# Layer 0's opening by halves of the features: the first modulation, x and the input weights in two halves, with four weight units between them

## The chip, the cores and the metric

The kernel runs on one core of one Trainium2 chip. The metric is the device time of one execution in microseconds (us); the figure compared is the median of the runs. A profile is one execution recorded by the hardware, with every instruction's start and end on TensorE (PE), VectorE (DVE), ScalarE (ACT), GpSimd (POOL) and the DMA queues.

## The reference

It is a two-layer decoder trunk in fp32 with 256 tokens and 1024 features. What matters here is the start of layer 0:

```
mod = silu(c) @ w_ada[l] + b_ada[l]          # 1024 x 6144 per layer
shift1, scale1, gate1, shift2, scale2, gate2 = split(mod, 6)
h = x * (1 + scale1) + shift1
z = h @ w_in                                 # 1024 x 1984: q 256, kv 128, key 64, then 3 x 512 channels
...                                          # attention from the first 448, gated conv from the channels
y = concat(rms(attn), rms(conv)) @ w_o
x = layer_norm(alpha * x + gate1 * y)
h = x * (1 + scale2) + shift2
f = swiglu(h)  (layer 0)   or   top-2 of 8 experts  (layer 1)
x = layer_norm(alpha * x + gate2 * f)
```

## The kernel before

All weights stream through a ring of seven slots of 2 MB in SBUF, `raw[0..6]`. The order of the loads is the list `loads`; the SyncE queue issues them in that order (L486 to L492) and waits, for each, until the load seven places earlier has been released by its reader. `w_ada` comes as strips `("ada", l, n)` of 512 rows by one vector of 1024 columns, two strips for each of the six vectors of a layer; `w_in` comes as `wa` (the 448 columns of the attention inputs) and as `wb`, `wc`, `wu` (512 channel columns each); then come `qkv`, `oc` and `oa`.

Modulation. VectorE multiplies each strip row block (128 rows by 1024 columns) by a per-partition value of silu(c) and adds it to an accumulator `ada_acc` (`ada_part`, L1063, the instruction at L1082; the text calls one of them a sum). The accumulator begins as the bias, written by ScalarE (`ada_init`, L648). After the eight sums of a vector TensorE adds over the partitions: by one-column products (`early_sums`, L1749) for the first two vectors, by a product with ones for the gates (L1731), by transposes (L1729) for the others, whose blocks ScalarE then adds up (`drain_ada`, L660). The results pass one after another through PSUM bank 7, in the order of the list `BANK7`. For strips 1 and 2 TensorE also takes over the fourth row block (`early_rows`, L1742). `unread` issues eight products of 512 columns (L1756) whose results nobody reads.

After both vectors, TensorE turns x (`turn_input`, L1773), ScalarE and VectorE modulate it into `h_t` (L682, L1100), and TensorE forms the low-rank part with `wa` in fp32 (L1815). The channel blocks are formed from two-part splits: for each of twelve weight units (128 x 1024) ScalarE makes the high part in one of three buffers `w_mix` (L732), VectorE the low part (L1187), and TensorE does 24 products (`channels`, `three`, L1794 to L1796), after which the buffer is free. The same is done for the modulated input in two halves (`halve`: L739, L1192). VectorE's stream has in between: an angle table (L1153 to L1168), the scaling by the norms and the rotary key (L1217 to L1226), and the strip sums of the later vectors, placed by hand with `sums`. After the units come the product `cu` (L1241), convolution, scores (L1898), softmax, the output products for the conv rows (L1918) and the attention rows (L1957), and the feed-forward, whose first product is L1971.

Of the kernel before, what the change touches and what calls it, by code (L numbers as in the profile page):

```python
# [28 lines left out]
P = 128  # L29
# [52 lines left out]
BANK7 = [("ada", 0, 0, 0), ("ada", 0, 1, 0), "params"]  # L82
PE_ROWS = (1, 2)
BANK7 += [("ada", 0, 2, 0), ("ada", 0, 2, 1), ("ada", 0, 3, 0), ("ada", 0, 3, 1), ("ssq_conv", 0), ("ssq_attn", 0), ("ada", 0, 4, 0), ("ada", 0, 4, 1)]
# [13 lines left out]
HALVED = EARLY + 1  # L98

MIX_UNITS = 12  # L100
MRING = 3
MIX_ADA = (((5, 6), (7,), (8, 9)), ((), (9, 10), (11,)))
MIX_FIRST, MIX_LATE = ((4, 5, 6, 7), (9,)), ((8, 9), (10, 11))
# [23 lines left out]
def trunk(nc, a, out):  # L127
    with ExitStack() as ctx:
# [5 lines left out]
        def sem(name):  # L134
# [32 lines left out]
        c_col = sb("c_col", [P, KC])  # L167
# [95 lines left out]
        hx_hi, hx_lo = (hx_hi0, hx_hi1), (hx_lo0, hx_lo1)  # L263
        rp_k = cu[:, 0, 2:].rearrange("p (k t r) -> p k t r", k=4, t=TT)
# [38 lines left out]
        half_full = [sem(f"half_full{k}") for k in range(HALVED)]  # L303
# [4 lines left out]
        prm_loaded, x_loaded, ln_loaded, rt_loaded = (sem("prm_loaded"), sem("x_loaded"), sem("ln_loaded"),  # L308
                                                      sem("rt_loaded"))
# [49 lines left out]

        def win_src(l, lo, hi):  # L360
            return a["w_in"][l][:, lo:hi].rearrange("(c p) n -> p c n", p=P)
# [3 lines left out]
        def load_ada(l, n):  # L365
            k = ADA_ORDER.index(("ada", l, n))
            src, parts = strip_src(l, n), 2 if k < EARLY else 1
            loads.append((("ada", l, n), [(q * SLOT // parts, (q + 1) * SLOT // parts, 4 // parts,
                                           src[:, q * 4 // parts:(q + 1) * 4 // parts, :]) for q in range(parts)],
                          (bank7_full, BANK7.index(("ada", l, n // 2, 0)) + 1) if k < EARLY else (ada_summed, k + 1)))  # L370

# [3 lines left out]
        for n in range(4):  # L375
            load_ada(0, n)
        for l in range(L):
            z0 = ZA
            if l == 0:
                load_pe(("wa", l), [(h * 4 * ZA, (h + 1) * 4 * ZA, 4, win_src(l, 0, ZA)[:, 4 * h:4 * h + 4, :]) for h in range(2)],  # L380
                        (za_mm, TT * (l + 1)))
            else:
                load_pe(("wa", l), [(0, KC * ZA, KC, win_src(l, 0, ZA))], (za_mm, TT * (l + 1)))
            load_pe(("wb", l), [(0, SLOT, KC, win_src(l, z0, z0 + D_CONV))], (mix_used, MIX_UNITS * l + 4))
            if l == 0:
                load_ada(0, 4)
            load_pe(("wc", l), [(0, SLOT, KC, win_src(l, z0 + D_CONV, z0 + 2 * D_CONV))], (mix_used, MIX_UNITS * l + 8))
            for n in MIX_ADA[l][0]:
                load_ada(l, n)
            load_pe(("wu", l), [(0, SLOT, KC, win_src(l, z0 + 2 * D_CONV, z0 + 3 * D_CONV))], (mix_used, MIX_UNITS * l + 12))  # L390
            for n in MIX_ADA[l][1]:
                load_ada(l, n)
            load_pe(("qkv", l), [(0, 2 * 768, 2, a["w_uq"][l].rearrange("(c p) n -> p c n", p=P)),
                                 (2 * 768, 2 * 768 + 1024, 1, a["w_ukv"][l].rearrange("(c p) n -> p c n", p=P))], (v_mm, l + 1))
            for n in MIX_ADA[l][2]:
                load_ada(l, n)
            load_pe(("oc", l), [(0, SLOT, 4, a["w_o"][l][512:1024, :].rearrange("(c p) n -> p c n", p=P))],
                    (yc_mm, 3 * (l + 1)))
            load_pe(("oa", l), [(0, SLOT, 4, a["w_o"][l][0:512, :].rearrange("(c p) n -> p c n", p=P))],
                    (ya_mm, 2 * TT * (l + 1)))  # L400
            if l == 0:
# [55 lines left out]
        def chunk_ready(v, t, c):  # L457

            if v >= 1 and t == 0:
                return ht_ready, HT[v] + c + 1  # L460
# [169 lines left out]
        def _(act):  # L630
# [85 lines left out]
            def mixer(l):  # L716
# [9 lines left out]
                def unit(n):  # L726
                    name, at, g = mix_weight(l, n)
                    if at == 0:
                        wait_load(act, name)
# [1512 lines left out]
```

## Time and profile before

| | |
|---|---|
| median of 3 runs | 1418.36 us (1417.6 to 1418.51) |
| span of the profiled execution | 1415.7 us |
| TensorE busy | 1390.7 us |
| VectorE busy | 1251.7 us |
| ScalarE busy | 1012.6 us |
| HBM read | 475.67 MB, 340 GB/s over the span |

The profiled execution's own time is not given apart from its span; the span runs from its first to its last instruction and is 2.7 us below the median of the runs. All moments in the text are in us from the start of the span. A busy engine is one with an instruction in flight; idle time carries the name of what ended it.

### The profile page before, as it was taken

The numbers are of one execution on the slowest core, as the hardware profiler recorded it, in microseconds if no ns is written. First come the engines' busy times: TensorE is split into PE (matmuls) and PEld (weight loads), VectorE is DVE, ScalarE is ACT, GpSimd is POOL, SyncE is SP. The second block draws the span as 40 slices with busy tenths as digits, with TensorE's granted clock in tenths as the row PEclk, the third lists the DMA queues.
The fourth block names the chain that finished last, engine by engine and source line by source line (L and its number), as shares of the span: only waits on it lengthen the run. The fifth ranks groups of instructions, "written<-read, shape, count | busy, mean of one in ns | idle before, by whom it ended". The sixth has DMA issues, their size and how long they took to land.

```text
span 1415.7 us, 20150 instructions
## 1 busy us (share of the span) xinstructions
PE 1390.7 (98%) x7013; PEld 1149.1 (81%) x7013; DVE 1251.7 (88%) x1388; ACT 1012.6 (72%) x1286; POOL 63.3 (4%) x123
## 2 busy tenths in 40 slices
PE   6999999999999999999999999999999999999996
PEld 4876999997967888888888888888888888888885
DVE  5987888876799989998998899999889899899998
ACT  2453544454355888888988888888898888888884
POOL 1000000000013500000000000000000000001000
PEclk9999999999999999999999999999999999999998
DMA  9996398977564999999999999999999999999970
GB/s 361 416 412 240 143 349 290 378 282 276 207 258 171 385 369 366 392 380 375 379 393 365 366 398 367 380 383 387 367 379 392 365 371 392 387 362 390 413 306 32
DMA packets 203472, 482.16 MB, mean 341 GB/s; under 512 B 6944, under 2 KB 31630, under 8 KB 203418
## 3 DMA queue, kind: packets, MB, share of 16 engines
q1 hardware_dynamic: 198848, 470.31, 88.1%
q0 software_dynamic: 1584, 5.77, 1.0%
q10 hardware_dynamic: 2986, 5.38, 1.0%
q8 instruction: 32, 0.52, 0.1%
q14 instruction: 22, 0.18, 0.0%
HBM read 475.67 MB, written 5.77 MB: 340 GB/s over the span
## 4 chain that ended last, share of the span: by engine, by line
PE 96%; DVE 2%; DMA 1%; ACT 0%; issue 0%; POOL 0%; SPq 0%; ACTq 0%; DVEq 0%; POOLq 0%
PE ps L1794 27%; PE ps L1796 27%; PE ps L1795 27%; PE ps L1957 2%; PE ps L2144 2%; PE ps L1815 2%; PE ps L1918 2%; PE ps L1971 1%; PE ps L1756 1%; DMA raw<-in_w_ada_dram 1%; PE ps L1731 1%; PE ps L1867 0%; PE ps L2094 0%; PE ps L1773 0%; PE ps L1729 0%; PE ps L1898 0%
## 5 line engine op out<-in xcount | busy, mean ns | idle before, releaser
L1424 DVE TENSOR_TENSOR low<-raw,w_hi 128x1024 fp32r<-128x1024 f32 x448 | 531.6, 1218 | 24.4 <-ACT w_hi L853 16.2
L853 ACT ACTIVATE w_hi<-raw 128x1024 fp32r<-128x1024 f32 x448 | 470.2, 1061 | 84.3 <-PE ps L1796 79.4
L1795 PE MATMUL ps<-low,h_hi 128*128 128x512 f32 x904 | 351.9, 389 | 0.0
L1794 PE MATMUL ps<-w_hi,h_lo 128*128 128x512 f32 x680 | 269.5, 396 | 0.0
L1796 PE MATMUL ps<-w_hi,h_hi 128*128 128x512 f32 x680 | 265.3, 390 | 0.0
L1795 PE MATMUL ps<-low,hid_hi 128*128 128x512 f32 x528 | 205.7, 390 | 0.0
L1795 PEld LDWEIGHTS ps<-low,h_hi 128*128 128x128 f32 x904 | 169.9, 188 | 34.2
L1424 DVE TENSOR_TENSOR low<-raw,e_hi 128x1024 fp32r<-128x1024 f32 x112 | 136.7, 1220 | 19.8 <-ACT e_hi L853 19.8
L1796 PEld LDWEIGHTS ps<-w_hi,h_hi 128*128 128x128 f32 x680 | 127.6, 188 | 27.4
L1794 PEld LDWEIGHTS ps<-w_hi,h_lo 128*128 128x128 f32 x680 | 127.8, 188 | 24.9
L1424 DVE TENSOR_TENSOR low<-raw,hx_lo 128x1024 fp32r<-128x1024 f32 x112 | 136.5, 1219 | 3.7
L853 ACT ACTIVATE hx_lo<-raw 128x1024 fp32r<-128x1024 f32 x112 | 118.8, 1061 | 26.4 <-PE ps L1796 26.2
L1082 DVE SCALAR_TENSOR_TENSOR ada_acc<-raw,c_act,ada_acc 128x1024 f32<-128x1024 f32 x94 | 120.5, 1283 | 10.6 <-ACT ada_acc L648 8.3
L853 ACT ACTIVATE e_hi<-raw 128x1024 fp32r<-128x1024 f32 x112 | 118.8, 1061 | 10.0 <-PE ps L1796 10.0
L1795 PEld LDWEIGHTS ps<-low,hid_hi 128*128 128x128 f32 x528 | 99.2, 188 | 19.7
L1794 PE MATMUL ps<-h_hi,low 128*128 128x256 f32 x320 | 92.7, 290 | 0.0
L1796 PE MATMUL ps<-h_hi,w_hi 128*128 128x256 f32 x320 | 90.5, 283 | 0.0
L1795 PE MATMUL ps<-h_lo,w_hi 128*128 128x256 f32 x320 | 90.5, 283 | 0.0
L1794 PE MATMUL ps<-w_hi,hid_lo 128*128 128x512 f32 x224 | 87.9, 392 | 0.0
L1796 PE MATMUL ps<-w_hi,hid_hi 128*128 128x512 f32 x224 | 87.2, 389 | 0.0
L1351 DVE TENSOR_TENSOR h_t<-ps,sil 128x512 f32<-128x512 f32 x67 | 46.1, 688 | 26.7 <-PE ps L1796 14.1
L1795 PEld LDWEIGHTS ps<-h_lo,w_hi 128*128 128x128 f32 x320 | 61.3, 191 | 1.1 <-issue 1.0
(377 smaller groups left out, 2268.0 us busy)
## 6 DMA issues: line engine op xcount, KB each, us to landing
raw<-in_moe_w_gate_dram SPq DMA_DIRECT2D x56, 2048.0 KB, 8.5
raw<-in_moe_w_up_dram SPq DMA_DIRECT2D x56, 2048.0 KB, 8.6
raw<-in_moe_w_down_dram SPq DMA_DIRECT2D x56, 2048.0 KB, 8.7
raw<-in_w_ada_dram SPq DMA_DIRECT2D x20, 2048.0 KB, 12.7
raw<-in_w_in_dram SPq DMA_DIRECT2D x6, 2048.0 KB, 12.5
raw<-in_ffn_w_gate_dram SPq DMA_DIRECT2D x11, 1024.0 KB, 8.3
raw<-in_ffn_w_up_dram SPq DMA_DIRECT2D x11, 1024.0 KB, 10.9
raw<-in_ffn_w_down_dram SPq DMA_DIRECT2D x11, 1024.0 KB, 4.9
```

Of the source, the lines that this page charges most:

```text
L853: act.activation(e_hi[k % ERING], raw[moe_slot(m)][:, (k % 4) * UNIT:(k % 4 + 1) * UNIT], ACT.Copy).then_inc(unit_hi, 1)
L1082: ins = dve.scalar_tensor_tensor(acc, w[:, c, :], c_act[:, 4 * kh + c:4 * kh + c + 1], acc, ALU.mult, ALU.add)
L1351: dve.tensor_tensor(hid, ps[:, 1, :].rearrange("p (f n) -> p f n", f=4), sil[:, :].rearrange("p (f n) -> p f n", f=4), ALU.mult).then_inc( ...
L1424: dve.tensor_tensor(low[moe_slot(m)][:, part], raw[moe_slot(m)][:, part], e_hi[k % ERING].bitcast(F32), ALU.subtract).then_inc(unit_lo, 1)
L1731: m = pe.matmul(ps[:, 7, :], ones[:, :], acc[:, part * 512:(part + 1) * 512], start=True, stop=True)
L1794: pe.matmul(o, x_lo, hi, start=first, stop=False, skip_group_check=True)
L1795: pe.matmul(o, x_hi, lo, start=False, stop=False, skip_group_check=True)
L1796: return pe.matmul(o, x_hi, hi, start=False, stop=last, skip_group_check=True)
L1815: m = pe.matmul(ps[:, 4 + t, 0:ZA], h_t[:, c, t * P:(t + 1) * P], wa[:, c, :], start=(n == 0), stop=(n == KC - 1))
L1918: m = pe.matmul(ps[:, bank, :], cv_t[:, c, t * P:(t + 1) * P], oc[:, c, half * 512:(half + 1) * 512], start=(c == 0), stop=(c == CC - 1))
L1957: m = pe.matmul(ps[:, (4, 2)[t] + half, :], a_t[:, c, t * P:(t + 1) * P], oa[:, c, half * 512:(half + 1) * 512], start=(c == 0), stop=(c = ...
L2144: m = pe.transpose(ps[:, 2, f * P:(f + 1) * P], hid[:, f, :], ident[:, :])
```

## The change

- Strips 0 to 3 (`EARLY`) are cut differently: a strip now holds 512 rows of the first (or last) 512 columns of shift and scale together, as four loads of 128 rows each with a semaphore of its own. So after strips 0 and 1 both vectors are complete for feature groups 0 to 3, and after strips 2 and 3 for groups 4 to 7.
- The first block of such a pair is a tensor_scalar into the accumulator, without bias. The last block is summed in two halves, and TensorE's one-column products follow each of them.
- c and the first two biases are loaded as 24 rows by ScalarE's queue and turned by TensorE; the bias is added by VectorE when it reads bank 7.
- x is loaded in two column halves. `wa`, `wb` and `wc` are loaded in halves, the first halves before strips 2 and 3.
- TensorE forms the first half of the low-rank product, turns the second half of x into PSUM (ScalarE holds a copy in `h_t`), then does units 0, 1, 4 and 5, then the sums over the partitions of the second half, the second half of the low-rank product, and units 2, 3, 6 and 7.
- `early_rows` and `unread` are gone. The angle table comes after unit 3. ScalarE's router loads come after unit 11. Of the 24 sums of strips 4 to 9, eleven (before: sixteen) come before `cu`. The turning of vector 3 moves behind the second and the third group of conv rows.

Constants and load order of the diff:

```
-BANK7 = [("ada", 0, 0, 0), ("ada", 0, 1, 0), "params"]
-PE_ROWS = (1, 2)
+BANK7 = [("ada", 0, 0, 0), "params", ("ada", 0, 1, 0)]
...
+EARLY_AT = (0, 1, 5, 6)
+HALVED = (2, 3, 4)
...
+MIX_ORDER = ((0, 1, 4, 5, 2, 3, 6, 7, 8, 9, 10, 11), tuple(range(12)))
 MRING = 3
...
+        def early_src(half, kh):
+            src = a["w_ada"][0][kh * 512:(kh + 1) * 512, 0:2 * D].rearrange("(c p) (v n) -> p c v n", p=P, v=2)
+            return src[:, :, :, half * 512:(half + 1) * 512]
...
+            for n in EARLY_AT[0:2]:
+                for q in range(4):
+                    load_part(n, q)
+            load_x(0)
+            load_part(2, 0)
+            load_part(3, 0)
+            load_x(1)
+            load_part(4, 0)
+            for n in EARLY_AT[2:4]:
+                for q in range(4):
+                    load_part(n, q)
+            for n in HALVED:
+                load_part(n, 1)
...
+                load_ada(0, 4)
+                load_block(0, 2)
+                load_ada(0, 5)
+                load_ada(0, 6)
+                load_qkv(0)
+                load_ada(0, 7)
+                load_oc(0)
+                load_ada(0, 8)
+                load_oa(0)
+                load_ada(0, 9)
```

ScalarE's start, its first modulation and its order:

```
+            act.dma_start(first_rows[0:KC, :], a["c"].rearrange("a (k p) -> (a k) p", p=P)).then_inc(c_loaded, 16)
+            act.dma_start(first_rows[KC:3 * KC, :], a["b_ada"][0:1, 0:2 * D].rearrange("a (k p) -> (a k) p", p=P)).then_inc(c_loaded, 16)
...
+            act.wait_ge(c_turned, 1)
+            act.activation(c_act[:, :], ps[:, 6, 0:KC], ACT.Silu).then_inc(c_ready, 1)
...
                 halve(0)
+                unit(0)
+                unit(1)
                 if l == 0:
+                    unit(4)
+                    hold_second()
...
+                    ada_init(2)
+                    unit(5)
+                    modulate_first(1)
                 halve(1)
+                unit(2)
                 if l == 0:
+                    unit(3)
+                    unit(6)
                     ada_init(3)
```

VectorE:

```
+            def modulate_first(half):
+
+                use, cols = bank7(("ada", 0, half, 0)), slice(4 * half, 4 * half + 4)
+                dve.wait_ge(c_ready, 2)
+                dve.wait_ge(bank7_full, use + 1)
+                dve.tensor_tensor(modc[:, 0, 0:2, cols], ps[:, 7, 0:KC].rearrange("p (v k) -> p v k", v=2), bias_cols[:, :, cols],
+                                  ALU.add).then_inc(bank7_free, 1)
...
+                halve(0)
+                unit(0)
+                unit(1)
                 if l == 0:
-                    sums(first, 4)
+                    ada_part(0, 2, 0, 1)
+                    unit(4)
+                    ada_part(0, 2, 1, 3)
+                    unit(5)
+                    ada_part(0, 2, 3, 4)
+                    ada(0, 3)
+                    modulate_first(1)
+                halve(1)
+                unit(2)
                 unit(3)
-                unit(4)
+                if l == 0:
+                    angle_table()
+                    unit(6)
...
                     unit(n)
-                    if l == 0 and n == MIX_UNITS - 1:
-                        sums(first, 2)
-                    elif l == 0 or n >= 9:
+                    if l == 0:
+                        sums(first, (1, 2, 1, 1, 6)[n - 7])
...
-                sums(late, 1)
+                sums(late, 2 if l == 0 else 1)
...
-                sums(late, 2 if l == 0 else 4)
+                sums(late, 4)
```

TensorE:

```
+            pe.transpose(ps[:, 6, 0:3 * KC], first_rows, ident[0:3 * KC, 0:3 * KC]).then_inc(c_turned, 1)
...
+            early_sums(0, 0)
+            turn_first(0)
+            early_sums(0, 1)
...
+                if l == 0:
+                    for t in range(TT):
+                        compressed(t, 0, KC // 2)
+                    turn_first(1)
...
+                    channels(0, 0, (0, 1))
+                    pe.wait_ge(xt_held, 1)
+                    channels(4, 2, (0, 1))
+                    use_bank7(("ada", 0, 1, 0))
+                    early_sums(1, 0)
+                    early_sums(1, 1)
+                    wait_load(pe, ("wa", 0))
+                    for t in range(TT):
+                        compressed(t, KC // 2, KC).then_inc(za_mm, 1)
+                    channels(0, 0, (2, 3))
+                    channels(4, 2, (2, 3))
```

## Rows read from the trace of the kernel before

**Rows 1.** The page: engines' busy time, and the chain that ended last, by engine.
```profile
PE 1390.7 (98%) x7013; PEld 1149.1 (81%) x7013; DVE 1251.7 (88%) x1388; ACT 1012.6 (72%) x1286; POOL 63.3 (4%) x123
...
PE 96%; DVE 2%; DMA 1%; ACT 0%; issue 0%; POOL 0%; SPq 0%; ACTq 0%; DVEq 0%; POOLq 0%
```

**Rows 2.** Busy time by stretch: the first row names the columns.
```profile
core 0: us, PE busy (x) PEld busy (x) DVE busy (x) ACT busy (x) POOL busy (x), PEclk, DMA share, GB/s
9.30:29.00 19.70, 18.10 (x64) 10.88 (x65) 17.88 (x14) 2.19 (x3) 0.00 (x0) 0.84 1.04 406
...
60.00:82.20 22.20, 21.50 (x179) 21.53 (x180) 20.01 (x17) 7.24 (x10) 0.00 (x0) 1.00 1.03 419
82.20:118.60 36.40, 36.38 (x154) 24.18 (x153) 33.18 (x65) 20.99 (x52) 6.17 (x5) 1.00 0.92 358
118.60:133.80 15.20, 15.20 (x50) 7.64 (x49) 10.32 (x19) 5.71 (x24) 0.00 (x0) 1.00 0.59 209
```

**Rows 3.** The chain that ended last, in order of time: start, length, what.
```profile
10.48 7.28 PE ps L1756 x10
...
33.21 12.04 PE ps L1815 x32
...
53.55 0.48 DVE zn L1217
...
56.70 1.29 DVE ada_acc L1082
...
82.17 0.86 PE ps L1731 x2
...
93.38 0.22 PE ps L1898 x2
...
121.74 0.44 PE ps L1729 x4
...
133.80 6.25 PE ps L1971 x56
```

**Rows 4.** VectorE in order of time: start, length, what, idle time before it.
```profile
9.29 13.12 DVE L1082 SCALAR_TENSOR_TENSOR ada_acc<-raw,c_act,ada_acc 128x1024 f32<-128x1024 f32 x10 [8.35 <-ACT ada_acc L648]
...
37.07 0.22 DVE L1153 CAST slot_no<-slot_i 128x128 f32<-128x128 int32 x1
...
40.70 0.23 DVE L1168 TENSOR_SCALAR ang<-ang 128x128 f32<-128x128 f32 x1
...
115.68 2.94 DVE L1082 SCALAR_TENSOR_TENSOR ada_acc<-raw,c_act,ada_acc 128x1024 f32<-128x1024 f32 x2
```

**Rows 5.** DMA issues of the first 150 us: size, median us to landing.
```profile
c_col<-in_c_dram SPq DMA_DIRECT2D x1, 4.0 KB, 2.6
pos_i<-in_positions_dram ACTq DMA_DIRECT2D x1, 1.0 KB, 8.5
```

**Rows 6.** TensorE and its weight loads (PEld) in order of time, 15 to 24 us.
```profile
15.74 0.33 PEld L1756 LDWEIGHTS ps<-raw,ident 128*128 128x128 f32 x1 [0.52 <-issue]
16.31 0.19 PEld L1756 LDWEIGHTS ps<-raw,ident 128*128 128x128 f32 x1 [0.24 <-issue]
16.74 0.19 PEld L1756 LDWEIGHTS ps<-raw,ident 128*128 128x128 f32 x1 [0.24 <-issue]
...
21.64 2.51 PE L1742 MATMUL ps<-c_act,raw 128*128 128x1 f32 x16 [0.42 <-ACT modc L665]
```

**Rows 7.** Busy time and granted clock (third number from the end) by 1 us.
```profile
22.00:23.00 1.00, 1.00 (x11) 1.00 (x10) 0.41 (x1) 0.63 (x1) 0.00 (x0) 0.92 1.03 401
...
24.00:25.00 1.00, 1.00 (x2) 0.49 (x3) 0.96 (x2) 0.00 (x0) 0.00 (x0) 0.50 1.06 413
...
29.00:30.00 1.00, 1.00 (x7) 0.96 (x6) 0.00 (x0) 0.00 (x0) 0.00 (x0) 0.66 1.06 407
```

**Rows 8.** Groups of instructions by shape: count, busy us, mean ns.
```profile
L1187 DVE TENSOR_TENSOR low<-raw,w_mix 128x1024 fp32r<-128x1024 f32 x12 | 14.6, 1222 | 0.5 <-ACT w_mix L732 0.2
...
L1129 DVE TENSOR_SCALAR yv<-yv,meanvar,rstd 128x1024 f32<-128x1024 f32 x2 | 1.6, 812 | 0.1
```

More of the change, by code:

```diff
@@ L366, in load_ada @@
             k = ADA_ORDER.index(("ada", l, n))
[L367 to L370, printed above, removed]
+            if k < EARLY:
+                src = early_src(n // 2, n % 2)
+                loads.append((("ada", l, n), [(q * D, (q + 1) * D, 2, src[:, q]) for q in range(4)],
+                              (bank7_full, BANK7.index(("ada", 0, n // 2, 0)) + 1)))
+            else:
+                loads.append((("ada", l, n), [(0, SLOT, 4, strip_src(l, n))], (ada_summed, k + 1)))
@@ L489, in _ @@
                     sp.wait_ge(s, value)
[L490 to L495 removed]
+                for q in range(len(loads[n][1])):
+                    load_part(n, q)
             def expert_loads(i, e, first, store):
@@ L671, in modulate @@
             def modulate(v, l, row, last, t):
[L673 to L678 removed]
+                act.wait_ge(fold_ready, v)
+                shift, scale = modf[:, v, 0, :], modf[:, v, 1, :]
                 tok = slice(t * P, (t + 1) * P)
[L680 removed]
+                for c in range(KC) if t == 0 else ACT_C:
                     act.wait_ge(xt_mm, TT * KC * v + KC * t + (c | 3) + 1)
@@ L1134, in _ @@
             dve.wait_ge(c_ready, 1)
-            for n in range(4):
-                ada(0, n)
+            ada(0, 0)
+            ada(0, 1)
             def residual(k, t):
@@ L1807, in mixer, with compressed @@
                 wa = slot_of(("wa", l))[:, 0:KC * ZA].rearrange("p (c n) -> p c n", c=KC)
-                for t in range(TT):
-                    for n, c in enumerate(range(KC)):
-                        if l == 0 and t == 0 and c == KC // 2:
-                            wait_load(pe, ("wa", l))
-                        if l == 1 and t == 0 and n == 6:
+                def compressed(t, first, last):
+                    for c in range(first, last):
+                        if l == 1 and t == 0 and c == 6:
                             turn_input(2, 1)
@@ L1815, in mixer, with channels @@
                         m = pe.matmul(ps[:, 4 + t, 0:ZA], h_t[:, c, t * P:(t + 1) * P], wa[:, c, :],
-                                      start=(n == 0), stop=(n == KC - 1))
-                    m.then_inc(za_mm, 1)
-                def channels(first, bank):
-                    for k in range(4):
+                                      start=(c == 0), stop=(c == KC - 1))
+                    return m
+                def channels(first, bank, ks=range(4)):
+                    for k in ks:
                         name, at, g = mix_weight(l, first + k)
```

344 lines of the change are left out of this document (183 added, 161 removed).

## The prediction

> **What bounds the kernel now.** I read the page first. TensorE is busy in 98% of the span and carries 96% of the chain that ended last [rows 1], so time taken out of the opening should reach the end, unless transfers or another engine are the limit there. The busy time by stretch of layer 0's mixer shows which limit holds when [rows 2]. Up to 82 us the DMA engines are full at 406 to 419 GB/s; from 118.6 they are at 59%, so they stop being a limit before the feed-forward starts. VectorE is busy for 33.2 of the 36.4 us from 82.2 to 118.6. That is what the reader should see there: in the attention part VectorE is nearly as full as TensorE.
>
> The chain gives the milestones [rows 3]: TensorE's first product starts at 10.5, when the first strip has landed; the low-rank product (L1815) starts at 33.2 and takes 12.0; the channel products end at 82.2; scores start at 93.4; the products that turn modulation vector 4 (L1729) stand at 121.7, and the feed-forward (L1971) starts at 133.8. Lastly VectorE in order of time [rows 4]: strip sums run at 1.31 us each (13.12/10), and they began at 9.3 only because ScalarE was 8.35 us late with the bias.
>
> **The change, part by part.** Times are us of the profiled execution (span 1415.7); the median of the runs, 1418.36, lies 2.7 above it, and I carry that difference over unchanged.
>
> *The first sums.* The bias no longer seeds the first accumulators, so the 8.35 us wait goes. Instead c and the biases of shift and scale come as rows through a transpose on TensorE. The nearest rows are far apart: c landed 2.6 after its issue, the positions 8.5 [rows 5]. Both new loads are issued at the very start, like c, so I take 3 to 4 for them and about 6 for the start of the sums; the other end is kept for a rival. Strips 0 and 1 are 4.2 MB. The first 2.1 MB were there at 10.4, and at 0.406 MB/us [rows 2] the last part lands at 15.65. Seven of the eight sums are done as their parts land; the eighth comes in two halves (0.75 each), so half 1 is ready at 16.45 and half 2 at 17.15.
>
> *To the first product.* TensorE is at half speed here. A one-column product costs 0.157 there (2.51/16) [rows 6], so each group of eight takes 1.25; eight transposes of x at 0.22 (twice the 0.44/4 of L1729 [rows 3]) take 1.7: 16.45 + 1.25 + 1.7 + 1.25 = 20.65. The bias addition (0.3) and one modulation (0.55) bring 21.5. Before it was 33.2: 11.7 earlier, with four of the eight feature groups.
>
> *The half product, at which clock.* Without the unread products nothing dense precedes it. 16 instructions at 0.376 (12.0/32 [rows 3]) are 6.0. The trace has two dense starts. From 10.5 six instructions take until 15.74 (0.87 each), then the pace is 0.43 [rows 6]. From 24.0 the granted clock is 0.50, the lower level of 1.2 GHz, and it rises within 29 to 30 [rows 7]. The one-column products in between did not keep the clock: it fell in the slice 22 to 23. I take the same 5.3 at the lower level, of which half is lost: 6.0 + 2.5 = 8.5, ending at 30.0. Bounds: nothing lost, and the loss twice (both are rivals). The Trainium skill (TensorE: Matmul & The Clock Gate, Terms) prices throttled time at half of it, and counts the engine as throttled until it has worked; it speaks against dropping the unread products. By it the price is the same 2.6.
>
> *Between the halves.* Turning x's second half and the parameters takes 1.1: 31.1. A weight unit is 24 products at 0.12 (21.5/179 [rows 2]), 2.9, so unit 0 is used up at 34.0. Only then may ScalarE write its buffer for unit 5 (three buffers): 1.05 more, 35.1. VectorE by then: from 21.9 it waits 1.1 for ScalarE's copy, takes 3.5 for the residue and units 0 and 1 (1.22 each [rows 8], 0.07 less back to back), waits 0.55 for strip 2, takes 0.8 for the first sum, now a tensor_scalar (as L1129 [rows 8]), 1.15 for unit 4 and 2.6 for two sums: 31.6. It waits 3.5; this wait is new. Unit 5 and five sums follow (1.2 + 6.7): half 1 at 42.3, half 2 at 43.0. TensorE ends its four units at 34.0 + 8.65 = 42.65, then has sixteen one-column products at 0.117: 44.5. Modulation from the held copy: 45.2. Second half product at full clock: 51.2.
>
> *From there VectorE sets the pace.* ScalarE's copy is ready at 46.9; VectorE has the second residue, units 2 and 3, the angle table (moved here, 3.9 [rows 4]) and unit 6: 46.9 + 1.2 + 2.3 + 3.9 + 1.1 = 55.4. Scaling by the norms and the rotary key take 3.4 (53.3 to 56.7 [rows 3]): 58.8, and 59.1 with unit 7's wait for ScalarE, whose additional table load is hidden by the angle table. Then five units (5.7) and eleven sums (14.4): 79.2. TensorE alone would be at 76.1 (51.2, eight units of 2.9, 1.3 of transposes, 0.4 of waits), against 82.2. So the channels end 6.1 earlier, but the product cu, which VectorE does next, comes only 3.0 earlier. From cu to the last strip sum VectorE was busy 33.2 [rows 2], and gaps between linked instructions add 0.6. The change leaves thirteen sums there where eight were, five more, 6.5: 79.2 + 33.2 + 0.6 + 6.5 = 119.5. Before, the last sum ended at 118.6 [rows 4], and its reader L1729 stood at 121.7 only because TensorE was late. Now TensorE, itself held up by VectorE at the scores and the probabilities, is there at about 118.2 and waits until 119.5. Gain: 121.7 - 119.5 = 2.2. From there to 133.8 it is TensorE's own 12 us; VectorE keeps about 1 us of slack.
>
> *Costed at nothing.* The new order of the loads: by cumulated bytes at 0.41 MB/us wu lands at 54 (used at 60), strip 6 at 64 (used at 75), the query weights at 68 (used at 77), the output blocks at 79 and 89 (used at 93 and 114). If this cover went, each us would be one on TensorE. The third feed-forward block is issued at 131 instead of 119 and used after 145. The router loads, moved behind unit 11, issue while ScalarE waits. Removing the unread products and those on the strips' last rows gives nothing more by itself: TensorE waited for VectorE behind them. The drains of vector 3 move into later idle time of ScalarE; the scores lose 1.1 of turning between them, which the probabilities' wait for VectorE takes back.
>
> Sum: 133.8 - 2.2 = 131.6, and 1418.36 - 2.2 = 1416.2. That is 0.16%, just inside the 0.2% (2.8 us) that I take as the least that a measurement of this kernel tells from nothing.
>
> **Rivals.**
> - *Full clock early.* The light work from 16.5 on suffices, or the clock rises soon. Unit 0 is used up to 2.5 earlier and VectorE's 3.5 wait shrinks to 1.0: gain 4.7, 1413.7. For it: two dense starts are few to go by. Against: one-column products lost the clock.
> - *TensorE stays the bound.* If VectorE waits less than I count, all 6.1 of the channels come through: 1412.3. Against: 33.2 busy of 36.4, and five sums more.
> - *Clock lost again between the halves.* The second half product takes 2.5 longer, its norms reach VectorE at 57.2 instead of 55.4, and unit 7 comes 2.2 later: gain 0, 1418.3. The fall in slice 22 to 23 [rows 7] came after 5 us of one-column work, against 2.5 here, which speaks against it. The Trainium skill (same page, HAM oscillation) has pauses between bursts of products bring the clock down; by that this rival would hold.
> - *The rows of c come late (the other side).* If they take what the positions took, with issue and transpose the sums start at 11.9 and half 2 is ready at 11.9 + 0.8 + 6 x 1.31 + 1.5 = 22.1, 4.9 later, and all of it comes through: 2.7 slower, 1421.1. It is a loss from a start at 9.2 on, and one over 0.2% from 12.0 on. Against: they are issued before the queue fills.
>
> **How the numbers follow.** The forecast has 0.45 (own range 1414.6 to 1417.8: 1.6 either way for landings and waits of VectorE), full clock early 0.22, TensorE the bound 0.10, clock lost again 0.15, late rows 0.08. Over 0.2% faster: nearly all of the two fast cases (0.31) and a quarter of the forecast's (0.11): 0.42. Over 0.2% slower: half of the late rows and 0.03 for a late transfer: 0.07. Within 0.2%: 0.51. The range leaves out the worse part of the late rows and half of TensorE as the bound: 1412.5 to 1419.6.
>
> **What would show it.** First L1815 near 21.5, its first instructions 0.75 apart; VectorE idle about 3.5 ahead of unit 5; second half product from 45 to 51; TensorE through with the channels near 76 and VectorE with its sums at 79; VectorE hardly idle from 59 to 119; vector 4's first L1729 waiting for VectorE; first L1971 at 131.6. I am wrong if the sums start after 9, if the second half product runs at the lower clock, or if TensorE is found waiting for w_in or w_o.

## The result, and the profile after

The changed kernel takes 1420.97 us (median of 20 runs, 1418.23 to 1421.84), the kernel before, run beside it, 1417.96 (20 runs, 1417.07 to 1418.80): a ratio of 1.0019, with a 95% interval of 1.0013 to 1.0024. The change made the kernel 3.0 us slower, where I forecast 2.2 faster. The profiled execution has a span of 1419.1 us, 3.4 more than before. In every other execution here the time is 1.7 to 2.0 us above its span; by that the profile before, with its span of 1415.7, is of an execution of 1417.4 to 1417.7 (an estimate), somewhat under its median, which accounts for most of the difference between 3.4 and 3.0.

First the chain that ended last, in order of time: start, length, what.

```profile
13.07 1.30 DVE ada_acc L1177
...
15.71 0.76 DVE ada_acc L1173
16.61 1.84 PE ps L1860 x8
18.45 1.81 PE ps L1869 x8
20.26 1.51 PE ps L1860 x8
22.77 7.92 PE ps L1917 x16
30.70 0.87 PE ps L1869 x8
43.19 1.88 PE ps L1860 x16
45.93 7.95 PE ps L1917 x16
...
61.66 1.24 DVE low L1293
...
81.98 1.24 DVE cu L1355
...
94.52 2.11 DVE ada_acc L1177
...
121.96 1.30 DVE ada_acc L1177
124.02 3.44 PE ps L2080 x8
...
135.64 7.14 PE ps L2094 x64
```

The opening does what it should at its start: the sums are ready at 16.5, the low-rank product (L1917, before L1815) starts at 22.8 instead of 33.2 [rows 3]. But its two halves take 7.92 + 7.95, against 12.04 for the whole before, and the feed-forward (L2094, before L1971) starts 1.84 later than at 133.80. The chain has passed from TensorE to VectorE in between. The next view is the busy time and the granted clock (third number from the end) of single microseconds; the first row names the columns.

```profile
core 0: us, PE busy (x) PEld busy (x) DVE busy (x) ACT busy (x) POOL busy (x), PEclk, DMA share, GB/s
46.00:47.00 1.00, 1.00 (x3) 0.52 (x4) 0.43 (x2) 0.48 (x1) 0.00 (x0) 0.82 1.01 418
47.00:48.00 1.00, 1.00 (x3) 0.53 (x2) 0.39 (x1) 1.00 (x2) 0.00 (x0) 0.50 1.00 393
50.00:51.00 1.00, 1.00 (x4) 0.52 (x3) 1.00 (x1) 1.00 (x2) 0.00 (x0) 0.98 1.06 406
442.00:443.00 1.00, 1.00 (x4) 0.63 (x5) 0.93 (x5) 0.56 (x1) 0.00 (x0) 0.79 1.03 422
443.00:444.00 1.00, 1.00 (x2) 0.34 (x1) 0.93 (x6) 0.00 (x0) 0.00 (x0) 0.50 0.30 119
```

Ahead of its last microseconds, where it falls in both kernels, the clock falls twice, each time to 0.50 (1.2 GHz): inside the second half product, at 46.6 (0.82 is the mean of a slice of which 0.36 is at half speed), and at 442.6 at layer 1's router. In the kernel before the first fall was in 22 to 23 [rows 7] and there was none at the router (1.00 in 442 to 444). VectorE in order of time:

```profile
35.75 1.23 DVE L1293 TENSOR_TENSOR low<-raw,w_mix 128x1024 fp32r<-128x1024 f32 x1 [3.58 <-ACT w_mix L808]
...
45.17 0.17 DVE L1191 TENSOR_TENSOR modc<-ps,cq_t 128x8 f32<-128x8 f32 x1 [1.51 <-PE ps L1860]
...
56.47 0.18 DVE L1331 RECIPROCAL rrms<-rms 128x4 f32<-128x4 f32 x1 [0.46 <-ACT rms L846]
...
61.66 1.23 DVE L1293 TENSOR_TENSOR low<-raw,w_mix 128x1024 fp32r<-128x1024 f32 x1 [1.63 <-ACT w_mix L808]
...
93.14 3.48 DVE L1177 SCALAR_TENSOR_TENSOR ada_acc<-raw,c_act,ada_acc 128x1024 f32<-128x1024 f32 x2
...
118.01 5.24 DVE L1177 SCALAR_TENSOR_TENSOR ada_acc<-raw,c_act,ada_acc 128x1024 f32<-128x1024 f32 x4
```

The 3.58 ahead of unit 5 is the wait that was forecast (3.5). The 1.63 ahead of unit 7 is the late second half product at work: ScalarE's copy of unit 7 waits for its buffer. The last sum ends at 123.25; before, at 118.6 [rows 4].

At the router TensorE goes on with three unread products (six instructions, L1876), here with the products just before them:

```profile
439.79 2.33 PE L2184 MATMUL ps<-router_w,h_t 128*128 128x8 f32 x16 [0.17 <-ACT h_t L746]
442.04 0.38 PE L2185 MATMUL ps<-router_b,ones 1*128 1x8 f32 x2
442.36 4.54 PE L1876 MATMUL ps<-gate,ident 128*128 128x512 f32 x6
```

They took 2.84 in the kernel before. From the feed-forward's start to the first product of L2225 (before, L2102), which stands behind the routing, it is 313.2 us now (135.64 to 448.87) and 311.9 before (133.80 to 445.66): 1.4 of the 3.4 us is lost there, 1.84 in the opening.

### The profile page after: what moved, and what is told of

Read it like the earlier page. It is cut to its first block, busy times and chain, and to the rows that moved or that the text cites. A ratio compares the mean times of both kernels' runs of the same rounds, so it can differ in the third digit from the quotient of the medians.

```text
span 1419.1 us, 20079 instructions
## 1 busy us (share of the span) xinstructions
PE 1382.5 (97%) x6966; PEld 1144.2 (81%) x6966; DVE 1254.0 (88%) x1391; ACT 1010.9 (71%) x1281; POOL 64.5 (5%) x123
## 4 chain that ended last, share of the span: by engine, by line
PE 93%; DVE 5%; ACT 1%; DMA 1%; issue 1%; SPq 0%; POOL 0%; DVEq 0%; ACTq 0%; POOLq 0%
PE ps L1897 27%; PE ps L1899 27%; PE ps L1898 27%; PE ps L1917 2%; DVE ada_acc L1177 2%; PE ps L2267 2%; PE ps L2080 2%; PE ps L2094 1%; PE ps L2037 1%; DMA raw<-in_w_ada_dram 1%; PE ps L1876 0%; PE ps L2217 0%; PE ps L1847 0%; PE ps L1860 0%; PE ps L1845 0%
## 5 line engine op out<-in xcount | busy, mean ns | idle before, releaser
L945 ACT ACTIVATE hx_lo<-raw 128x1024 fp32r<-128x1024 f32 x112 | 118.8, 1061 | 26.5 <-PE ps L1899 26.3
```

Of the source, the lines that this page charges most:

```text
L945: act.activation(e_hi[k % ERING], raw[moe_slot(m)][:, (k % 4) * UNIT:(k % 4 + 1) * UNIT], ACT.Copy).then_inc(unit_hi, 1)
```

## The experiments

The edits are against the kernel after, unless said otherwise. In the table "diff" is the median less that of the kernel before run beside it (1417.96 beside after, then 1417.94 for e1 to e4, 1417.62 for e5 to e8, 1417.54 for e9 to e12, 1418.14 for e13 and e14), and what an edit brought is the difference of two such numbers. FF is the start of the first feed-forward product in the profiled execution, read from TensorE in order of time (which puts it 0.17 ahead of the chain). Last stands where the clock fell up to FF, and where at the router. FF and the falls are of one execution each, and that execution can be far from its kernel's median: under it by 2.0 in e9, 1.8 in e2, 1.5 in e7 and 1.3 in e10 and e12, above it by 1.6 in e11, and within 0.5 in the others.

```
kernel                        median (runs), us             diff  ratio, 95%        FF      falls; at the router
before                                                                              133.63  22.8; none
after                         1420.97 (1418.23 to 1421.84)  +3.0  1.0013 to 1.0024  135.47  46.6; 442.6
e1  filling between halves    1420.12 (1419.26 to 1421.37)  +2.2  1.0007 to 1.0026  135.06  118.7; 443.0
e2  filling at the start      1416.66 (1414.71 to 1417.79)  -1.3  0.9982 to 1.0000  130.75  114.9; none
e3  unit 5 moved behind       1419.48 (1418.67 to 1421.15)  +1.5  1.0004 to 1.0022  134.00  none; 441.4
e4  three sums fewer          1419.06 (1417.47 to 1420.36)  +1.1  1.0000 to 1.0018  133.68  45.9, 117.5; 441.8
e5  bank 7 sooner             1420.70 (1420.14 to 1421.69)  +3.1  1.0012 to 1.0031  135.80  47.2; 443.2
e6  router, 2 unread          1419.99 (1419.12 to 1423.60)  +2.4  1.0012 to 1.0033  135.76  47.3; 443.2
e7  before, 2 unread          1419.19 (1417.58 to 1420.84)  +1.6  1.0001 to 1.0019  133.86  23.3; none
e8  e2 + e3 + e5              1419.67 (1418.06 to 1420.53)  +2.1  1.0004 to 1.0022  134.26  38.5; 441.3
e9  e2 + e5                   1416.97 (1414.92 to 1418.38)  -0.6  0.9987 to 1.0005  129.75  none; 437.0
e10 before, three sums fewer  1416.85 (1415.18 to 1418.36)  -0.7  0.9985 to 1.0003  131.84  21.3; none
e11 dense product in router   1421.26 (1419.40 to 1423.21)  +3.7  1.0015 to 1.0033  135.25  46.6; 442.5
e12 four unread at the start  1418.41 (1416.71 to 1418.70)  +0.9  0.9994 to 1.0012  131.59  43.0; 438.9
e13 before, layer 1 later     1421.08 (1419.71 to 1423.45)  +2.9  1.0013 to 1.0031  133.26  20.5; 443.7
e14 after, layer 1 later      1423.90 (1423.14 to 1425.18)  +5.8  1.0027 to 1.0055  135.51  47.1; 446.5
```

**e1, one unread product between the halves.**

```
                     early_sums(1, 1)
+                    unread(1, slot_of(("wa", 0)))
```

> The changed kernel with one unread product of 512 columns (two instructions, 0.86 us at full clock) on TensorE after the second half's one-column products, where it waits 0.9 us for the modulated input anyway. The changed kernel takes 1421.0, the one before 1418.0. Clock theory: the second half product took 7.95 instead of 6.0 because TensorE had only one-column products and waiting from 43.1 to 45.9; with dense work in the wait the granted clock stays at 1.00 in more of the executions, the product takes 6.0, unit 7 comes 2 us earlier, and the time falls to 1419 to 1419.5. Rival, VectorE alone sets the pace after the second half (as my prediction had it for a short loss): the product gets faster, the time stays at 1421. Second rival: one product is too little, the clock falls as before, time 1421 and the same 7.9.

The clock stayed at 1.00 from 46 to 50, and the second half product took 6.25. Still only 0.4 us reached the feed-forward, and 0.8 the median, with intervals that overlap. TensorE in order of time shows where the rest went:

```profile
46.10 6.25 PE L1922 MATMUL ps<-raw,h_t 128*128 128x448 f32 x16
...
117.36 0.58 PE L2074 MATMUL ps<-ones,h_t 128*128 128x1 f32 x4 [1.56 <-ACT ps L728]
```

Behind that wait of 1.56, for bank 7's drain, the clock fell (at 118.7), and eight products that take 3.44 in the kernel after took 5.24. A short fall cost about 1.7 at both places (7.95 against 6.25, and 5.24 against 3.44), and here it was gone at one light place and stood at the next.

**e2, the opening filled ahead of the first half product.** Four unread products on part 3 of strip 0, and one before the low-rank product.

```
+            pe.wait_ge(early_full[0][3], 16)
+            unread(4, slot_of(("ada", 0, 0)))
             early_sums(0, 0)
             turn_first(0)
             early_sums(0, 1)
+            pe.wait_ge(half_full[2], 16)
+            unread(1, slot_of(("wa", 0)))
```

> The changed kernel with the unread products back at the start: four (eight instructions) once strip 0 is in, about 10.1, and one more after the first half's sums over the partitions. Clock theory: the sixteen one-column products and eight transposes, 5.2 us in the changed kernel (0.23 each), take 3.0 at full clock, so the first half product starts at about 20.6 instead of 22.8 and takes 6.0 to 8 instead of 7.9; unit 5's low part comes 2 to 4 earlier, VectorE's wait of 3.6 before it shrinks to under 2, and the time falls by 2 to 4, to 1417 to 1419. Rival, loads set the opening: strips 2 and 3 hold VectorE up instead, first half earlier but unit 5's chain gains under 1: 1420 or more.

4.3 us faster than after, and the one version whose interval against before does not reach above 1, if only just (its upper end is 1.0000). TensorE from the opening on:

```profile
10.19 6.51 PE L1867 MATMUL ps<-raw,ident 128*128 128x512 f32 x8 [3.83 <-DMA raw<-in_w_ada_dram]
16.54 1.01 PE L1860 MATMUL ps<-ones,ada_acc 128*128 128x1 f32 x8
17.41 1.07 PE L1874 MATMUL ps<-ident,x_sb 128*128 128x128 f32 x8
...
20.29 6.25 PE L1926 MATMUL ps<-raw,h_t 128*128 128x448 f32 x16
...
113.48 5.38 PE L2089 MATMUL ps<-raw,cv 128*128 128x512 f32 x8
```

The one-column products take 1.01 instead of 1.84, the transposes 1.07 instead of 1.95, the product 6.25 instead of 7.92, and it ends 4.2 earlier (26.5 against 30.7). VectorE's wait ahead of unit 5 falls from 3.58 to 0.36, and cu comes 5.9 earlier (76.12 against 81.98). At 114.9, behind the same wait for bank 7, the clock falls for the first time. The eight products there take 5.38, so TensorE, not VectorE, is late for vector 4 (118.69, where the last sum ended at 117.4), and 1.3 of the 5.9 go.

**e3, unit 5 behind the second vector's sums, two strip sums ahead of it.**

```
TensorE:
-                    channels(4, 2, (0, 1))
+                    channels(4, 2, (0,))
                     use_bank7(("ada", 0, 1, 0))
                     early_sums(1, 0)
                     early_sums(1, 1)
+                    channels(4, 2, (1,))
VectorE:
-                    ada_part(0, 2, 1, 3)
+                    ada_part(0, 2, 1, 4)
+                    ada_part(0, 3, 0, 1)
                     unit(5)
-                    ada_part(0, 2, 3, 4)
-                    ada(0, 3)
+                    ada_part(0, 3, 1, 4)
```

> The changed kernel with unit 5 moved: on TensorE after the second half's one-column products (three units before them, one behind, which covers the modulation), on VectorE behind two more strip sums, where it waited 3.6 us for unit 5's high part. Chain theory: VectorE no longer waits, its sums of the second half end near 41.5 instead of 43.6; the modulation and the copy run under unit 5; dense products stand ahead of the second half product, which therefore takes 6.0; it ends near 52 instead of 53.9, VectorE is 2 earlier too, and the time falls by 2, to about 1419. Rival: the two engines were balanced, what one gains the other loses, and the time stays within 0.5 of 1421.

24 products now stand between the light ones and the second half product, which took 6.18 with the clock up. The wait ahead of unit 5 went to 2.03. FF came 1.5 earlier, and the median fell as much, though its interval overlaps that of after. In this profile real products stood where e1 had its unread one, and the clock stayed up as well.

**e4, three of VectorE's strip sums left out**, two of strip 5 and one of strip 6; what they would add is missing in the output.

> The changed kernel, leaving out three strip sums (row blocks 1 and 2 of strip 5, row block 1 of strip 6) between unit 10 and the product cu, so that gate 1 and shift 2 of layer 0 lack these rows. VectorE theory: from unit 7 to the last sum VectorE sets the pace, so 3.9 us less work there shows nearly in full until TensorE binds: TensorE ends its channel products at 78.6 and waited for qr_t at 91.1 by 1.5; then the sums of vector 4 come 3.9 earlier against a TensorE that is 1.6 to 2.5 earlier: the time falls by 1.5 to 2.5, to 1418.5 to 1419.5. Rival, TensorE's chain binds from the second half product on (the lost clock alone explains the loss): under 0.7 less, 1420.3 or more.

cu came 3.7 earlier (78.31 against 81.98) and then waited 0.86 for TensorE, so up to there VectorE had set the pace by 2.8. Of that only 1.8 reached FF, and 1.9 the median, as the clock fell once more, at 117.5 (the eight products took 5.24).

**e10, the same three sums left out of the kernel before,** with the same gap in the output.

> The kernel before, without the three strip sums that e4 leaves out of the kernel after (the output lacks those rows). Taking them out of the kernel after brought the feed-forward forward by 1.8 us. Theory, that the kernel before has slack on VectorE and the kernel after none: less than 0.3 us of change here, 1417.6. Rival, that VectorE bounds this stretch in both: the same 1.8 us, 1416.0, and then the new order did not make VectorE the limit.

Also 1.8 at FF (131.84 against 133.63), and 0.7 in the median, with an interval that holds no change. So my theory that the kernel before has slack there falls in its plain form. In the profile 0.7 of the 1.8 is there before the first sum left out (the low-rank product starts at 32.36 instead of 33.05, as the clock fell at 21.3 and not at 22.8 in an opening that the edit does not touch), and 1.1 is the wait of TensorE for VectorE at 60.7, which is gone:

```profile
60.70 0.36 PE L1794 MATMUL ps<-hx_hi,low 128*128 128x256 f32 x1 [1.06 <-DVE low L1187]
```

That row is the kernel before's. It had 1.1 us to give there, after which VectorE waits 2.02 for ScalarE's copy at 65.4. At cu, VectorE waits 1.95 for TensorE in both (80.40 in e10, 82.20 before). So VectorE holds TensorE up at one place in the kernel before; the kernel after gave 3.7 at cu, where VectorE did not wait at all.

**e5, bank 7 drained sooner:** vector 3's second product and its drain ahead of the last convolution rows, on TensorE and ScalarE.

```
+                if l == 0:
+                    ada(0, 3, 1)
                 conv_rows(1, 1, 6).then_inc(yc_mm, 1)
-                if l == 0:
-                    ada(0, 3, 1)
```

> The changed kernel with one move: the second turn of vector 3 stands on TensorE before the last group of conv rows instead of behind it, and its drain on ScalarE before those rows too. In the changed kernel TensorE waits 1.56 us at 117 for this drain of bank 7, and in two of the first experiments the clock fell to 0.50 right behind this wait (L1957's counterpart took 5.2 instead of 3.4). Bank theory: the wait goes, no fall follows, and where the clock would have fallen 1.7 us come back: 1419.5 to 1420.3 against 1421.0 of the changed kernel. Rival, VectorE's last strip sum ends at 123.25 whatever TensorE does, 0.7 after TensorE is ready: the time stays at 1420.5 to 1421.

Nothing gained. The wait of 1.56 went and came back in front of vector 4, now for VectorE's sum:

```profile
123.72 0.63 PE L1845 MATMUL ps<-ident,ada_acc 128*128 128x128 f32 x4 [1.55 <-DVE ada_acc L1177]
```

**e9, e2 with e5's edit.**

> The kernel after with the opening filled as in e2 (four unread products before the first sums, one before the first half product), and with vector 3's second product and its drain ahead of the last convolution rows. In e2 TensorE waited 1.56 us for bank 7 at 111.5, its clock then fell, and vector 4's products at 118.7 waited for TensorE, not for VectorE, whose last sum had ended at 117.4. Theory: without that wait the clock stays up and vector 4 starts at about 117.4, 1.3 us earlier than in e2, so 1415.4. Rival, that the pace is VectorE's there in any case, as it was where the same edit was made without the filled opening: 1416.7, as e2.

By the profile the theory held: the eight products took 3.70, vector 4 stood at 117.67 instead of 118.69, and FF at 129.75, the earliest of all. It waited for VectorE again, 1.55, so 1.0 and not 1.3. But the clock then fell at 437.0, at the router, where it had not in e2's profile, and the medians (-0.6 and -1.3) don't tell the two apart.

**e12, e2 without the one unread product ahead of the first half product.**

> e2 without the unread product ahead of the first half product: only the four before the first sums stay. Theory, that one-column products and transposes alone let the clock fall again (it fell after 5 us of them in the kernel before and after 3 in the kernel after): the low-rank product starts at full clock and is throttled on its way or soon after, and 1.5 to 2.5 of the 4.3 us that e2 brought are lost: about 1418.5. Rival, that early dense work is what counts and the short stretch of light work behind it does no harm: as e2, 1416.7.

It lost 2.2 of e2's 4.3. The first half product ran at full clock (6.25), so it was not there that the clock was lost; the second half product was hit (43.0 to 46.4, 7.95), and with it VectorE's unit 7, which waited 1.63 again. My guess of the size was right and that of the place wrong.

**e8, e2, e3 and e5 together.**

> The changed kernel with the unread products at the start, unit 5 moved behind the second half's sums, and vector 3's second turn sooner. Clock theory: the gains of the start (4.3) stays, the order adds what VectorE and TensorE no longer wait for each other (1 to 1.5), the bank wait goes (0.5 to 1.5): 1413.8 to 1415.5, faster than the kernel before by 2.5 to 4. Rival, from cu on VectorE binds and strips 2 and 3 are still on their way at 36: the start alone takes all there is, 1416 to 1416.7.

3.3 slower than e2 alone. TensorE in order of time:

```profile
38.68 3.54 PE L1860 MATMUL ps<-ones,ada_acc 128*128 128x1 f32 x16 [2.63 <-DVE ada_acc L1173]
```

With unit 5 moved and the opening early, TensorE runs out of work at 36.0 and waits 2.63 for VectorE's sums. The clock falls at 38.5 and stays down until 45.4; the one-column products take 3.54 instead of 1.92, VectorE waits 3.13 for them, and cu is at 80.76 instead of 76.12. Alone, e2 and e3 had gained, and e5 had done nothing.

**e6 and e7, the router's three unread products cut to two, in after and in before** (`warm(3, 1, 1)` becomes `warm(2, 1, 1)`).

> The changed kernel with two instead of three unread products at the router of layer 1. In its profile the clock was at 0.50 there from 442.8 to 446, the three took 4.5 us instead of 2.8 and TensorE came 1.4 later to the routing products than VectorE had them ready. Router theory: with two, TensorE is through in 3.0 at either clock, the 1.4 goes, and the time is 1419.6 to 1420. Rival, the fall there is rare or is moved to the products behind: no change, 1421.

> The kernel before with the same edit at the router. Its profile has the clock at 1.00 there. If the fall at the router belongs to the changed kernel, nothing is gained here: 1418.0, or a little more as the clock may now fall behind the shorter filling. If the fall comes in part of the executions of either kernel, this one gains too, up to 1, and its spread (1416.8 to 1418.5) narrows.

In after the clock fell all the same (443.2), and the 0.6 gained lies within the intervals, so the third product is not what brings the fall there. In before the runs got 1.6 longer, and e7's profile does not show why: it is of the second fastest execution (1417.69, where the median is 1419.19). In it the filling is followed by a wait of 0.94 for VectorE, but the routing products stand 5.49 behind the start of the router's last block, where they stood 5.48 behind it before, so nothing was lost at this place. Ten of the eleven executions have a mean granted clock of 0.991 to 0.993, where those of the kernel before have 0.993 to 0.995. So with the shorter filling this kernel was more often at the lower clock; at which place is not shown.

**e11, one dense product amid the router's sixteen narrow ones.**

```
+                    if t == 1 and c == KC // 2:
+                        warm(1, 1, 1)
                     pe.wait_ge(*chunk_ready(3, t, c))
```

> The kernel after with one unread product more, in the middle of the router's second block of 16 narrow products in layer 1. Theory: the narrow products lose the clock, the unread ones behind them then take 4.5 us instead of 2.8; one dense product among them keeps it, at 0.4 us of its own: 1.0 us faster, 1419.9, and the granted clock is 1.0 from 440 to 450. Rival, that the clock falls with the phase and not with the light work: it falls all the same, and the time is 0.4 us longer, 1421.3.

In the profile the theory failed:

```profile
440.83 1.10 PE L1876 MATMUL ps<-gate,ident 128*128 128x512 f32 x2
441.77 1.02 PE L2186 MATMUL ps<-router_w,h_t 128*128 128x8 f32 x8
442.73 0.59 PE L2187 MATMUL ps<-router_b,ones 1*128 1x8 f32 x2
443.25 5.49 PE L1876 MATMUL ps<-gate,ident 128*128 128x512 f32 x6
```

The clock fell at 442.5 all the same, and stayed down until 449.3, twice as long as in after (442.6 to 446.0). The product also cost twice what I expected, as it is two instructions of 0.43. This profile is of one of the slowest executions (1422.87). The four fastest of the eleven, 1419.40 to 1419.96, have a mean granted clock of 0.997, which none of after's 20 reaches (0.996 at most). They may be executions in which the clock stayed up, as the theory had it; no profile shows one, and by the median nothing was gained.

**e13 and e14, layer 1 moved back as a whole:** four more unread products at the start of its mixer, in before and in after (`warm(2, 2, 1)` becomes `warm(6, 2, 1)`).

> The kernel before with four unread products more at the start of layer 1's mixer, where TensorE never waits: they cost 4 x 0.44 = 1.8 us and push all that follows back by as much, past the place in time at which the kernel after reaches its router. Theory, that the router's clock falls by the moment at which it is reached: the fall now comes here too, 1.8 + 1.5 = 3.3 us slower, 1420.9. Rival, that the fall belongs to something in the program of the kernel after: 1.8 slower, 1419.4, and the granted clock stays at 1.0 from 435 to 450.

> The kernel after with the same four unread products at the start of layer 1's mixer. Theory of the moment: the router is reached 1.8 us later, the fall may go, and 1.8 - 1.5 = 0.3 us is left: 1421.2. Rival, that the fall belongs to the program: it stays, 1422.8.

The expectation priced the shift wrongly. A product of 512 columns is two instructions of 0.43 and not one, so four cost 3.4. The first row is the kernel before's, the second e13's:

```profile
330.90 1.88 PE L1762 MATMUL ps<-gate,ident 128*128 128x512 f32 x4
330.53 5.31 PE L1762 MATMUL ps<-gate,ident 128*128 128x512 f32 x12
```

As waits behind them took up part of it, the layer is 2.9 us later against its own start. The router's last block starts at 440.51, where it was 437.94 before; in e14 it starts 3.0 later than in after. The runs lost just that: 2.9 in e13 and 2.8 in e14. Only the profile of e13 shows more than the shift, a router like that of the kernel after:

```profile
440.51 2.33 PE L2061 MATMUL ps<-router_w,h_t 128*128 128x8 f32 x16 [0.17 <-ACT h_t L682]
442.78 0.38 PE L2062 MATMUL ps<-router_b,ones 1*128 1x8 f32 x2
443.09 4.54 PE L1762 MATMUL ps<-gate,ident 128*128 128x512 f32 x6
```

So the old program can meet the fall at the router too. That the shift brought it is not shown. The loss in the runs leaves no room for 1.4 us more than in the kernel before, and some executions of the kernel before may have the fall as well: its 110 executions beside e1 to e14 lie in two groups, 54 below 1417.86 with a mean granted clock of 0.994 or 0.995, and 56 from there on, 47 of them with 0.993. The medians of the groups are 0.9 apart, and its profile is by its span of the faster one. In the kernel after the same shift did not take the fall away (446.5 to 449.9, the filling 4.38). Nor does a simple threshold in time fit: in e4 the router's last block started at 438.07 and the clock fell, in e7 at 438.17 and it did not.

## Why the prediction was wrong

**The step that failed** is "Second half product at full clock: 51.2". It ran at the lower clock and ended at 53.88. That was the rival "clock lost again between the halves", which I had given 0.15 and a gain of 0. I argued that 5 us of one-column work had come before the fall of [rows 7] and there would be only 2.5 here. 2.8 were enough, 1.9 of such products and a wait of 0.9. I had named this as a sign of being wrong. The Trainium skill (TensorE: Matmul & The Clock Gate, HAM oscillation) has pauses between bursts bring the clock down, and by it I had named this rival. The trace agrees in the outcome (0.82 in 46 to 47, 0.50 behind it) but only in part in the cause: the pause was 0.9 us, far shorter than the waits for data in the page's example. e1, e3 and e2, each in its own way, kept the clock there, and the product took 6.18 to 6.25.

From the forecast's 131.6 for L2094 to the measured 135.64 it is 4.0, and it can be laid out along the chain:

- *Light work at half speed*, 0.7. Eight one-column products took 1.84 and 1.51 (0.19 to 0.23 each), where I took 0.157 from a row that held both clock levels; the transposes 1.81 (0.227, I had 0.22). The first product came at 22.77 instead of 21.5. It took 7.92 instead of 8.5, so 0.6 of the 1.3 came back.
- *The clock in the second half product*, 1.9. VectorE's norms came 1.1 later (56.47, forecast 55.4), and unit 7 another 1.5 later for its ScalarE copy: 61.66 instead of 59.1, of which 0.7 is the first point. The rival had 2.2 for unit 7 and a gain of 0 in all; that it came out 1.8 worse at the feed-forward lies in the other terms here.
- *VectorE from 61.7 to cu*, 0.2: the sixteen operations took 20.3, forecast 20.1.
- *VectorE from cu to the last sum*, 1.0: 41.3 instead of 40.3. By busy time (40.25 of 41.27) it is 0.55 more work and 0.4 more idle time than I had. The sum at 94.52 took 2.11 instead of 1.30, and the two operations of L1416 and L1417 from 112.98 took 1.75 and 1.63 instead of 1.22. Each of the three had begun while an addition of GpSimd was running. The sum at 93.14 began just ahead of such an addition and took its usual 1.28, and there the addition took 2.32, where it took 1.26 in the kernel before (its row stands below). The Trainium skill (GPSIMD Engine Reference, Specifications) has the two engines contend for the SBUF interface where VectorE reads two SBUF inputs; these are such operations, and the rows agree. I had summed durations of the lone engine; before, too, one pair took 2.94 instead of 2.6 [rows 4]. No run separates this term: that it is GpSimd is read from the overlap in the trace, not shown by an edit.
- *From there to the feed-forward*, 0.3 (12.4 instead of 12.1).

GpSimd's addition beside the sums at 93.14 and 94.52:

```profile
93.22 2.32 POOL L642 TENSOR_TENSOR h_t<-h_t 128x512 f32<-128x512 f32 x1 [88.61 <-ACT h_t L891]
```

**The other 1.4** of the profiled execution is the router's fall at 442.6, which the prediction didn't contain at all: it ended with "From there to 133.8 it is TensorE's own 12 us" and carried the gain at that point on to the end unchanged. The profile of e13 has the same fall in the kernel before, so it is not the change alone that makes it. How often either kernel meets it, and what decides it, stays open: a shorter filling does not take it away (e6), a dense product amid the narrow ones does not in every execution (e11), and a shift of 3.0 does not (e14). So how much of the median's 3.0 us comes from the router is not shown.

**"Nothing more by itself".** I costed the dropped unread products at 2.5 for the first half product and nothing otherwise. e2 puts them back in another place and gains 4.3. In the profiles that is 0.8 on each group of one-column products, 0.9 on the transposes and 1.7 on the product; the second half product then takes 1.7 less, and e12 shows that to hang on the one unread product right ahead of the first half. With them the sign of the result turns.

**What was right.** The rows of c were there by 5.9 and the halves by 16.46 and 17.1 (forecast 16.45 and 17.15). The loss in the first half product was of the kind forecast. VectorE's wait ahead of unit 5 was 3.58 (3.5), and the second half product's start 45.93 (45.2). VectorE did set the pace from 59 on: the last sum's reader waited for it, 0.39, and e5 and e9 found the same wait behind each edit of TensorE. "TensorE stays the bound" did not hold, nor "full clock early" by itself; the latter is what e2 makes true by force. With it the kernel comes to 1.3 us under the one before, where that rival had 4.7. No transfer bound anything where I had named its cover.

The forecast's effect was -2.2 and the measured one +3.0. In the profile (+3.4) the miss of 5.6 is 4.0 in the opening, 1.4 at the router, and 0.2 elsewhere.

## What to carry to other kernels

Where a dense product is split in two by light work (one-column products, small transposes, narrow router products), price each part at the lower clock until a run shows otherwise, and price the light work there too, at the rate of a row that lies wholly at that level. Before dropping unread products, look at what stands behind them: nothing waits for them, but the speed of the next dense work can rest on them. Judge such an edit on many runs and at all light places of the kernel, as a fall taken away at one place (e1, e9) stood at another, 70 and 320 us later. A profile is one execution: set its time beside the median before reading a difference of 1 or 2 us out of it. And where an edit is to shift a stretch, read the shift from the trace: mine was 2.9 and not 1.8.

## What the runs showed of the hardware

- The clock fell behind light work or a short wait, and TensorE could be busy all the time there. In e8 it fell at 38.5, in a wait of 2.63; in e2 at 114.9, 1.9 behind a wait of 1.56. At the router of the kernel after the busy share was 1.00 in 442 to 443, with 0.17 us of idle time in the 3 us ahead of the fall. What stood there was sixteen products of 8 columns.
- The stretches at half speed were of two lengths: 46.6 to 50.0 and 442.6 to 446.0 in after, 114.9 to 118.3 in e2, but 22.8 to 29.7 in before, 38.5 to 45.4 in e8 and 442.5 to 449.3 in e11. Dense work stood behind the last one as behind the short ones. A short one cost 1.7 us of dense work (7.95 against 6.25, 5.38 against 3.68, 4.54 against 2.84).
- The moment of a fall differs between executions of the same instructions. The opening is the same in before, e7, e10 and e13, and the clock fell there at 22.8, 23.3, 21.3 and 20.5. It is the same in after, e4, e5, e6, e11 and e14, and the clock fell at 46.6, 45.9, 47.2, 47.3, 46.6 and 47.1. The Trainium skill (TensorE: Matmul & The Clock Gate, What's actually happening) lets the chip's observation of activity run free of the kernel's start; by that the same program can fall in one execution and not in the next. The times are in line with it: the runs of e2 lie in two groups (five at 1414.7 to 1414.9 with a mean granted clock of 0.995 or 0.996, six at 1416.7 to 1417.8 with 0.993 or 0.994), 2 us apart, which is about the price of one fall. The kernel before has two such groups as well, 0.9 apart.
- One-column products cost 0.12 each at the upper clock and 0.19 to 0.23 at the lower. A strip sum took 1.28 to 1.30 us, also where GpSimd's addition began behind it, and 2.11 where that addition was already running.
